# Latent tokens laid out, loaded, summed and normed ahead of the context tokens

## What is computed

```python
m_l = silu(c) @ w_ada + b_ada          # shift, scale, gate ... of the latent tokens
m_c = silu(c_ctx) @ w_ada + b_ada      # the same for the context tokens
hl = rmsnorm(x, g) * (1 + sc1) + sh1   # 256 latent tokens x 1024
hc = rmsnorm(ctx, g) * (1 + csc1) + csh1
v  = [hl; hc] @ w_in[:, 3D:4D]         # values: 512 tokens x 1024
```

## Time and profile before

| | |
|---|---|
| median of 3 runs | 875.49 (875.2 to 875.95) |
| the profiled execution, its own time | 874.96 |
| its span in the profile | 873.1 |
| TensorE matmuls, busy | 863.6 (99%) |
| VectorE, busy | 641.5 (73%) |
| ScalarE, busy | 488.5 (56%) |
| mean DMA rate | 184 GB/s |

### The profile page before, as it was taken

How to read it: one execution, slowest core, us unless ns; L and a number is a source line. 1 busy time by engine, 2 the same in 40 slices (tenths; PEclk the granted TensorE clock), 3 DMA queues, 4 the chain that set the end, 5 groups by cost and what they waited for, 6 DMA issues and landing times.

```text
span 873.1 us, 16932 instructions
## 1 busy us (share of the span) xinstructions
PE 863.6 (99%) x6308; PEld 783.7 (90%) x6308; DVE 641.5 (73%) x1080; ACT 488.5 (56%) x769; POOL 0.2 (0%) x4
## 2 busy tenths in 40 slices
PE   8999999999999999999999999999999999999997
PEld 3688888888899999999998899999998899999996
DVE  3793899999997787877677897766577765555555
ACT  5433677777766664655557545555544664444443
POOL 0000000000000000000000000000000000000000
PEclk9999999999999999999999999999999999999999
DMA  9974444444447556565564654444465465555551
GB/s 343 408 285 158 145 146 146 143 144 144 160 143 252 185 202 242 170 216 186 175 191 143 196 193 146 150 165 146 145 218 171 140 200 195 185 192 185 180 188 48
DMA packets 45585, 160.90 MB, mean 184 GB/s; under 512 B 5216, under 2 KB 6624, under 8 KB 45408
## 3 DMA queue, kind: packets, MB, share of 16 engines
q1 hardware_dynamic: 43632, 156.43, 52.7%
q10 hardware_dynamic: 1904, 3.81, 1.3%
HBM read 159.16 MB, written 1.05 MB: 183 GB/s over the span
## 4 chain that ended last, share of the span: by engine, by line
PE 94%; DVE 2%; ACT 1%; DMA 1%; SPq 0%; issue 0%; DVEq 0%; ACTq 0%
PE bank L420 22%; PE bank L422 21%; PE bank L421 21%; PE bank L474 5%; PE bank L476 5%; PE bank L475 5%; PE bank L1224 2%; PE bank L1227 2%; PE bank L1225 2%; DMA tok<-in_tok 1%; PE bank L442 1%; PE bank L1315 1%; PE bank L1333 1%; PE bank L1195 1%; PE bank L1296 0%; DVE arena L657 0%
## 5 line engine op out<-in xcount | busy, mean ns | idle before, releaser
L414 DVE TENSOR_TENSOR w_lo<-raw,w_hi 128x1024 fp32r<-128x1024 f32 x244 | 295.2, 1223 | 118.0 <-ACT w_hi L407 117.9
L420 PE MATMUL bank<-h_hi,w_hi 128*128 128x256 f32 (+1 forms) x1168 | 350.1, 300 | 0.0
L422 PE MATMUL bank<-h_hi,w_lo 128*128 128x256 f32 (+1 forms) x1168 | 343.5, 294 | 0.0
L421 PE MATMUL bank<-h_lo,w_hi 128*128 128x256 f32 (+1 forms) x1168 | 343.4, 294 | 0.0
L407 ACT ACTIVATE w_hi<-raw 128x1024 fp32r<-128x1024 f32 x244 | 252.7, 1051 | 111.3 <-PE bank L422 82.9
L420 PEld LDWEIGHTS bank<-h_hi,w_hi 128*128 128x128 f32 x1168 | 219.5, 188 | 9.5 <-issue 0.8
L421 PEld LDWEIGHTS bank<-h_lo,w_hi 128*128 128x128 f32 x1168 | 220.3, 189 | 6.5
L422 PEld LDWEIGHTS bank<-h_hi,w_lo 128*128 128x128 f32 x1168 | 220.0, 188 | 5.8
L420 PE MATMUL bank<-y_hi,w_hi 128*128 128x256 f32 x304 | 87.0, 286 | 0.1
L421 PE MATMUL bank<-y_lo,w_hi 128*128 128x256 f32 x304 | 85.6, 282 | 0.0
L422 PE MATMUL bank<-y_hi,w_lo 128*128 128x256 f32 x304 | 85.5, 281 | 0.0
(11 more groups left out here) (272 smaller groups left out, 1100.5 us busy)
## 6 DMA issues: line engine op xcount, KB each, us to landing
raw<-in_stream SPq DMA_DIRECT2D x244, 512.0 KB, 3.4
arena<-in_ada SPq DMA_DIRECT2D x40, 512.0 KB, 7.2
xres<-in_ada SPq DMA_DIRECT2D x8, 512.0 KB, 3.3
tok<-in_tok SPq DMA_DIRECT2D x3, 512.0 KB, 7.7
con<-in_con ACTq DMA_DIRECT2D x1, 1472.0 KB, 7.1
xres<-in_tok ACTq DMA_DIRECT2D x1, 1024.0 KB, 10.1
out<-arena SPq DMA_DIRECT2D x4, 256.0 KB, 2.0
tok<-in_tok SPq DMA_DIRECT2D x2, 256.0 KB, 9.5
```

Source lines behind the costliest of these rows:

```text
L414: dve.tensor_tensor(w_lo[c.slot][:, :], raw[c.slot][:, :], w_hi[c.slot][:, :].bitcast(F32), ALU.subtract).then_inc(S("split_lo"), 1)
L420: pe.matmul(dst, hi_w, a_hi, start=start, stop=False, skip_group_check=True)
L421: pe.matmul(dst, hi_w, a_lo, start=False, stop=False, skip_group_check=True)
L422: return pe.matmul(dst, lo_w, a_hi, start=False, stop=stop, skip_group_check=True)
```

## The change

- The columns of `tok` are ordered by half first: 8 latent tiles of 256 columns, then 8 context tiles (also in the array given to the kernel). The pieces are latent k = 0-3, latent 4-7, context 0-3, context 4-5, context 6-7. The buffers `h_hi` and `h_lo` keep their old order.
- SP issues: `cc`, piece 0, tile 0, piece 1, tiles 1, 2, 3, `par`, chunk 0, pieces 2, 3, 4, and then as before.
- The sums: VectorE adds two tiles of 256 to two others within a piece, and TensorE sums what is left with products of 256 columns (`add_tokens`): four for the latent half, into bank 1, and four for the context half, into bank 2 (`context_sum`), each half with its own logarithm and root.
- VectorE norms all latent tiles, two at a time, before `quarter(0)`; the context tiles come one by one for k = 0 and 1, in pairs later. The counts of `h_hi` and `h_lo` are taken in the order (0, latent), (1, latent), (0, context), (1, context), by `made_at`.
- TensorE's chunk 0 is no longer a call of `values` but a list of `value_tile` (k by k and token tile by token tile), with the context sum behind the third, tiles 4 to 6 of the modulation behind the fourth, tile 7 behind the fifth, and the turn of rows 1 ahead of the last.
- The load of `xres`, much later, becomes a plain copy of the latent half.

```diff
@@ -121,7 +121,7 @@
-PIECES = (0, 2, 4, 6, 7, 8)
+PIECES = (0, 4 * T, 8 * T, 12 * T, 14 * T, 16 * T)
@@ -154,7 +154,17 @@
 def normed_at(k, half):
+    return half * KT + k + 1
+def made_at(k, half):
...
+def token_cols(k, half):
+    return slice((half * KT + k) * T, (half * KT + k + 1) * T)
@@ -689,7 +699,7 @@
             def load_tokens(n):
-                x = slice(PIECES[n] * TC, PIECES[n + 1] * TC)
+                x = slice(PIECES[n], PIECES[n + 1])
...
             def load_ada(i):
@@ -703,17 +713,17 @@
                     sp.wait_ge(S("split_lo"), n - RING + 1)
                 load(stream_in, n * P, n % RING)
+            load_tokens(0)
             load_ada(0)
+            load_tokens(1)
             load_ada(1)
-            load_tokens(0)
             load_ada(2)
-            load_tokens(1)
+            load_ada(3)
+            sp.dma_start(par[:, :], par_in).then_inc(S("par_in"), 16)
+            load_one(0)
             load_tokens(2)
-            load_ada(3)
             load_tokens(3)
             load_tokens(4)
-            load_one(0)
-            sp.dma_start(par[:, :], par_in).then_inc(S("par_in"), 16)
             for q in range(1, QUARTERS):
                 for i in range(4 * q, 4 * q + 4):
                     load_ada(i)
@@ -798,7 +808,7 @@
-                act.activation(h_hi[:, at:at + T], tok[:, at:at + T], ACT.Identity, scale=gain[:, k:k + 1],
@@ -808,14 +818,15 @@
             def square_piece(n):
-                x = slice(PIECES[n] * TC, PIECES[n + 1] * TC)
+                x = slice(PIECES[n], PIECES[n + 1])
...
             def log_sum(half):
+                act.wait_ge(S("tok_summed"), half + 1)
...
-                act.activation(rstd[:, x], psum[1][:, x], ACT.Ln, scale=1.0 / D, bias=eps).then_inc(S("tok_rstd"), 1)
+                act.activation(rstd[:, x], psum[1 + half][:, 0:T], ACT.Ln, scale=1.0 / D, bias=eps).then_inc(S("tok_rstd"), 1)
             def root(half):
@@ -823,20 +834,23 @@
                 act.wait_ge(S("tok_rstd"), 2 * half + 1)
                 act.activation(x, x, ACT.Exp, scale=-0.5).then_inc(S("tok_rstd"), 1)
-            for n in range(5):
-                square_piece(n)
-            copy_rows(0)
-            hi(act, Chunk(0))
-            act.wait_ge(S("tok_summed"), 4)
+            square_piece(0)
+            square_piece(1)
             act.wait_ge(S("eps"), 1)
             log_sum(0)
             root(0)
+            copy_rows(0)
+            hi(act, Chunk(0))
+            modulate_half(0, 0)
+            square_piece(2)
+            modulate_half(1, 0)
+            square_piece(3)
+            square_piece(4)
             log_sum(1)
-            modulate_half(0, 0)
             root(1)
             modulate_half(0, 1)
-            modulate(1)
             copy_rows(1)
+            modulate_half(1, 1)
             hi(act, Chunk(1))
             modulate(2)
@@ -960,7 +974,7 @@
-            act.dma_start(by_tile(xres[:, :]), by_tile(tok_in)[:, :, 0:T]).then_inc(S("xres_in"), 16)
+            act.dma_start(xres[:, :], tok_in[:, 0:KT * T]).then_inc(S("xres_in"), 16)
@@ -1197,11 +1211,19 @@
-            def token_sum(m):
-                pe.wait_ge(S("tok_added"), m + 1)
-                pe.matmul(psum[1][:, :], ones, wide[:, 2 * m * TC:(2 * m + 1) * TC], start=m == 0, stop=m == 3,
-                          skip_group_check=True).then_inc(S("tok_summed"), 1)
+            def add_tokens(bank, first, start, stop):
+                for m in range(2):
+                    last = pe.matmul(psum[bank][:, 0:T], ones, wide[:, first + m * T:first + (m + 1) * T],
+                                     start=start and m == 0, stop=stop and m == 1, skip_group_check=True)
+                return last
+            def context_sum():
+                pe.wait_ge(S("tok_added"), 4)
+                add_tokens(2, PIECES[2], True, False)
+                pe.wait_ge(S("tok_squares"), 5)
+                add_tokens(2, PIECES[4], False, True).then_inc(S("tok_summed"), 1)
             def turn_rows(q):
@@ -1210,41 +1232,56 @@
                     last = pe.transpose(psum[TURN_BANKS[q]][:, m * P:m * P + P], mod_rows[q][:, m * P:m * P + P], ident)
                 last.then_inc(S("mod_turned"), 1)
+            def value_tile(j, b, tile):
+                c, half = Chunk(j), j // 4
+                k = 2 * (j % 4) + b
+                x = slice(k * TC + tile * P, k * TC + (tile + 1) * P)
+                dst = psum[4 * half + tile][:, :]
+                hi_w, lo_w = (w[c.slot][:, b * 512:b * 512 + 512] for w in (w_hi, w_lo))
+                pe.wait_ge(S("split_hi"), c.n + 1)
+                pe.wait_ge(S("h_hi"), made_at(k, tile // 2))
+                pe.matmul(dst, h_hi[:, x], hi_w, start=k == 0, stop=False, skip_group_check=True)
+                pe.wait_ge(S("split_lo"), c.n + 1)
+                pe.matmul(dst, h_hi[:, x], lo_w, start=False, stop=False, skip_group_check=True)
+                pe.wait_ge(S("h_lo"), made_at(k, tile // 2))
+                last = pe.matmul(dst, h_lo[:, x], hi_w, start=False, stop=k == KT - 1, skip_group_check=True)
+                if k == KT - 1 and tile < 3:
+                    last.then_inc(S("v_bank"), 1)
+                return last
             def values(j, between={}):
-                c, half = Chunk(j), j // 4
-                pe.wait_ge(S("split_lo"), c.n + 1)
                 for b in range(2):
-                    k = 2 * (j % 4) + b
                     for tile in range(4):
-                        x = slice(k * TC + tile * P, k * TC + (tile + 1) * P)
-                        dst = psum[4 * half + tile][:, :]
-                        hi_w, lo_w = (w[c.slot][:, b * 512:b * 512 + 512] for w in (w_hi, w_lo))
-                        pe.wait_ge(S("h_hi"), 2 * k + 1 + tile // 2)
-                        pe.matmul(dst, h_hi[:, x], hi_w, start=k == 0, stop=False, skip_group_check=True)
-                        pe.matmul(dst, h_hi[:, x], lo_w, start=False, stop=False, skip_group_check=True)
-                        pe.wait_ge(S("h_lo"), 2 * k + 1 + tile // 2)
-                        last = pe.matmul(dst, h_lo[:, x], hi_w, start=False, stop=k == KT - 1, skip_group_check=True)
-                        if k == KT - 1 and tile < 3:
-                            last.then_inc(S("v_bank"), 1)
+                        last = value_tile(j, b, tile)
                         if (b, tile) in between:
                             between[b, tile]()
                 last.then_inc(S("multiplied"), 1)
-            ada(0, 2)
             warm(FILL[0])
-            ada(2, 3)
-            token_sum(0)
+            pe.wait_ge(S("tok_added"), 1)
+            add_tokens(1, PIECES[0], True, False)
+            ada(0, 1)
+            pe.wait_ge(S("tok_added"), 2)
+            add_tokens(1, PIECES[1], False, True).then_inc(S("tok_summed"), 1)
+            ada(1, 4)
             warm(FILL[1])
-            token_sum(1)
-            ada(3, 4)
-            token_sum(2)
             pe.wait_ge(S("con_in"), 16)
             turn_rows(0)
-            token_sum(3)
-            ada(4, 5)
             warm(FILL[2])
-            values(0, {(0, 1): lambda: ada(5, 8), (0, 3): lambda: turn_rows(1)})
+            value_tile(0, 0, 0)
+            value_tile(0, 0, 1)
+            value_tile(0, 1, 0)
+            context_sum()
+            value_tile(0, 1, 1)
+            ada(4, 7)
+            value_tile(0, 0, 2)
+            ada(7, 8)
+            value_tile(0, 0, 3)
+            value_tile(0, 1, 2)
+            turn_rows(1)
+            value_tile(0, 1, 3).then_inc(S("multiplied"), 1)
             values(1, {(0, 1): lambda: ada(8, 12), (1, 0): lambda: turn_rows(2)})
             values(2, {(0, 1): lambda: ada(12, 16), (1, 0): lambda: turn_rows(3)})
             for j in range(3, KT):
@@ -1710,24 +1747,21 @@
-            def norm_tokens(k):
-                x = tok[:, k * TC:(k + 1) * TC]
-                dve.tensor_tensor(x, x, rstd, ALU.mult).then_inc(S("tok_normed"), 2)
-            def norm_half(k, half):
+            def norm_tokens(k, half, n=2):
...
-                x = tok[:, k * TC + half * T:k * TC + (half + 1) * T]
-                dve.tensor_tensor(x, x, rstd[:, half * T:(half + 1) * T], ALU.mult).then_inc(S("tok_normed"), 1)
+                x = tok[:, (half * KT + k) * T:(half * KT + k + n) * T].rearrange("p (k t) -> p k t", k=n)
+                root = rstd[:, half * T:(half + 1) * T].unsqueeze(1).to_broadcast([P, n, T])
+                dve.tensor_tensor(x, x, root, ALU.mult).then_inc(S("tok_normed"), n)
             def shift_half(k, half):
...
-                at, gain, shift = (k * TC, gain_l, mod) if half == 0 else (k * TC + T, gain_c, mod_c)
-                dve.tensor_scalar(wide[:, at:at + T], tok[:, at:at + T], gain[:, k:k + 1], shift[:, k:k + 1], ALU.mult,
@@ -1738,9 +1772,9 @@
             def low_half(k, half):
...
-                dve.wait_ge(S("tok_shifted"), 2 * k + half + 1)
-                dve.wait_ge(S("h_hi"), 2 * k + half + 1)
```

(53 more changed lines are left out.)

## The result

The changed kernel took 878.69 us (median of 6 runs, 878.14 to 880.07), the kernel before 875.49 (6 runs, 875.2 to 876.36). The ratio is 1.0036, interval 1.0024 to 1.0048: 3.2 slower. The forecast was 879.6, with a range of 876.6 to 881.4. A "ratio" is that of a kernel's time to that of the kernel before, measured beside it, with its 95% interval.

The account below looks back on a forecast made before the run. TensorE, busy 99% of the span, was taken as the bound, so only the first 30 us count. 2.9 gained at the first matmul against stalls, sums and lone tiles gave 4.1 us slower: 879.6, range 876.6 to 881.4.

Parts of the forecast that it names:

- The latent path: Loads to first value products: latent sums, norms and gains run ahead; third value matmul at 18.38, 2.08 earlier.
- What is put behind it: TensorE from the first value product to chunk 1: displaced work and stalls, putting chunk 1's third matmul 4.1 us later.
- The lone tile and tile 4: Chunk 0 on TensorE: modulation tile 7 multiplied alone and tile 4 no longer ahead of the values; about 1.1.
- The wait on `copy_rows(1)`: Late chunk 0: context modulation of k = 1 stands on ScalarE behind that copy, which waits for tile 7; stall 0.60.
- The uncovered chunk 1: Start of chunk 1: a single value tile covers the second transposes, gains and remainder; stall of 1.76 in two pieces.
- the context sum: TensorE's stream in chunk 0: four sums of 256 columns with nothing to cover them; 2.04, between 1.0 and 2.3.
- the mark: Third matmul of chunk 1, whose shift is the forecast: from 28.53 to 32.67, 4.1 us slower.
- The covered chain: Rival, 12%: tile 7's copy and the second turn come early enough, late stalls 0.6 and 1.8 go; 877.2 to 877.7.
- the change doesn't reach the first product: Rival, 5%: something else holds gains at 17.6 and `h_lo` at 20.30, all put behind still comes; 6.2 slower, 881.7.
- The early start: Rival, 12%: TensorE waits for nothing after 17.07, only its work counts; chunk 1 +0.5, 876.0, at best 874.0.
- The cap of 1.6 by the loads: Limit on any gain: tile 11's load lands at 28.9 to 29.1, so no version can win more than 1.6.
- The clock: Rival, 6%: TensorE falls to 1.2 GHz at the start, context sums alone take 2.04 more; +6.2, 881.7.

Follow-up runs that it names:

- norms_late: The changed kernel with three of the four latent norms moved behind the latent subtraction of k = 1; 879.26 us.
- tiles_together: The changed kernel with modulation tile 7 multiplied with tiles 4 to 6 behind the fourth value tile, turn left late; 877.75 us, ratio 1.0022.
- turn_late_before: The kernel before with only the second turn moved ahead of the last value tile of chunk 0; 877.32 us, ratio 1.0018.
- turn_early: tiles_together with the second turn moved ahead of two more value tiles, behind the first tile on the context half; 875.43 us, ratio 1.0001.
- combined: turn_filled with context squares folded to one sum product, that product one value tile later, and three latent norms behind it; 874.51 us, ratio 0.9986.
- turn_filled: turn_early with six warming products instead of two ahead of the first value product; 875.9 us, ratio 1.0005.
- loads_back: The changed kernel with parameters and weight chunk 0 loaded behind the context tokens again, as in the kernel before; 880.84 us, ratio 1.0059.

## Why the prediction was right

**The latent path**: right, a little long. First and third matmul forecast at 17.07 and 18.38, measured 16.84 and 18.03. The quarter starts at 15.40 (15.63), with norms and transposes close together as forecast (15.40 and 15.22); norms_late shows that without three of the norms it is only 0.18 earlier. Part of the agreement is luck: the first token sum began at 8.79 and not at 9.21, in a range of starts of 1.1, and from its end to the first norm it was 1.20 (11.79 to 12.99) and not 1.0. The root broadcast over two tiles costs a norm 0.60 (2.50 for four).

**What is put behind it**: all of it is there, in its order. The wait for `h_lo` of k = 1, 0.36 (0.48). The lone tile and tile 4, 1.1 as forecast (tiles_together gives back 1.77 with the wait behind it, forecast 1.0 + 0.6). The wait on `copy_rows(1)`, 0.53 (0.60). The uncovered chunk 1, 1.7 (1.76), and turn_late_before and turn_early show it from both sides. The queues cost nothing, as taken.

**The term that was mis-sized** is the context sum: 2.04, twice the recorded length of a 512-column product, whose modelled end overlaps what follows. Four of 256 columns take 1.54 from the first to the next start (20.23 to 21.77), and four more cost 1.73. This 0.5, the first value product 0.23 earlier than forecast and some 0.1 in the steps between are the 0.8 between the mark forecast, 32.67, and measured, 31.85, and bring 4.1 to 3.3.

**The rivals.** The covered chain is refuted by the waits at 27.80, 30.66 and 31.51. That the change doesn't reach the first product is refuted by that product's start at 16.84. The early start doesn't pay as the change stands. With tile 7 and the turn moved it breaks even (turn_early), and it pays only in combined: the deciding point, `h_lo` of k = 2 at the end of chunk 0, was the right one. The cap of 1.6 by the loads was not tested; combined, 0.9 faster, is under it. The clock kept its full rate in the changed kernel's trace, but my argument for this, that no hole was as long as the one behind the last matmul, failed: with the same holes it fell in the profiled execution of turn_early, for 0.8, where I had given that rival 2.04.

## What the runs showed of the hardware

The profiled execution of turn_early, by stretches (TensorE clock is the third value from the end), and its timeline:

```profile
16.00:18.00 2.00, 0.54 (x2) 0.19 (x1) 1.93 (x7) 1.42 (x2) 0.00 (x0) 0.91 1.03 412
18.00:21.00 3.00, 2.82 (x7) 2.31 (x8) 2.33 (x6) 1.66 (x4) 0.00 (x0) 0.50 1.03 411
21.00:22.00 1.00, 1.00 (x6) 0.87 (x5) 0.00 (x0) 0.00 (x0) 0.00 (x0) 0.97 1.01 401
```

```profile
9.28 1.03 PE L1217 MATMUL bank<-wide,con 128*128 128x256 f32 x4
...
17.32 0.48 PE L1244 MATMUL bank<-w_hi,h_hi 128*128 128x512 f32 x1 [1.27 <-ACT h_hi L811]
18.18 0.80 PE L1246 MATMUL bank<-w_lo,h_hi 128*128 128x512 f32 x1 [0.38 <-DVE w_lo L424]
...
19.20 0.63 PE L1244 MATMUL bank<-w_hi,h_hi 128*128 128x512 f32 x1
19.63 0.63 PE L1246 MATMUL bank<-w_lo,h_hi 128*128 128x512 f32 x1
...
30.12 0.50 PE L1248 MATMUL bank<-w_hi,h_lo 128*128 128x512 f32 x1
```

TensorE had idled 1.27 ahead of 17.32 and 0.38 ahead of 18.18. From 18 to 21 the granted clock was 0.50, which is 1.2 GHz, and a step between value matmuls was 0.43 (19.20 to 19.63) instead of 0.234. First to mark was 12.80, against 12.04 at the full clock in turn_filled: the fall cost 0.8. loads_back shows the same behind 3.21 of idle time: a granted clock of 0.50 from 20 to 22, and a step of 0.43 (20.13 to 20.56).

The three long runs of turn_early took about 1.8 more than its others. In the one of them with a trace the fall is only part of it: its mark is 1.79 behind that of turn_filled (30.12 against 28.33), 0.76 by the clock and 1.04 by the start, since the first token sum began at 9.28 against 8.24. tiles_together had the same holes and six runs of ten at 1.4 more, at a mean granted clock of 0.997 against 0.999; with the first hole filled, none of eleven was at 0.997. That these six fell too is likely, but none of them has a trace. The profiled executions of the changed kernel and of tiles_together had the holes and kept their clock, so the same gap may or may not cost.

The Trainium skill (TensorE: Matmul & The Clock Gate, What's actually happening) has the clock fall behind an idle stretch. The traces agree that it falls; they show it with matmuls on both sides of a hole of 1.3, in some executions and not in others.

## What to carry to other kernels

On an engine that is full from some point on, an earlier start is worth only what is not put behind it: list what each moved instruction stood beside before, since the same columns of a sum cost 0.2 to 0.7 among load waits and 1.3 to 1.7 in the stream. The transposes and gains for the next chunk need their cover counted in matmuls: nine matmuls later cost 1.9 in the kernel before, and six later 1.2 in the changed one (13.24 against 12.04), so each matmul of lost cover cost about 0.2, nearly its own step of 0.234. Multiply modulation tiles together: the fourth beside three others cost 0.01, alone it cost 1.1. A filled hole took the longest executions away, but it is worth a trial, not a rule: the median fell by 0.8 in tiles_together, stayed within 0.1 in the changed kernel, and rose from 875.4 to 875.9 in turn_early. And compare kernels by a stretch that leaves out their start, if the start scatters by more than what is sought.
